# Delta rule of a hybrid encoder in fp32: where the projection's matmuls stand in levels 1 to 4 of the triangular inverse

## The reference

```python
proj = h @ w_in                                  # q, k, v, z of every head, and more
...
m = jnp.where(strict, jnp.einsum('bhncd,bhnsd->bhncs', k_beta, k) * decay, 0.0)
t_inv = lax.linalg.triangular_solve(eye + m, eye, lower=True, unit_diagonal=True, ...)
u = t_inv @ v_beta
w = t_inv @ (k_beta * jnp.exp(g)[..., None])
# then a scan over the chunks carries a 128 x 128 state through each head
```

## Time and profile before

| | us |
|---|---|
| median of 3 runs | 1468.76 (1468.46 to 1468.94) |
| the profiled execution | 1469.18 |
| its span, first to last instruction | 1467.4 |
| PE busy | 1424.6 (97% of the span) |
| DVE, ACT, POOL busy | 560.3, 579.1, 555.1 (38%, 39%, 38%) |

### The profile page before, as it was taken

One profiled execution on the slowest core, in us unless ns is written; L12 is line 12 of the kernel. 1 busy time (PEld: TensorE's weight loads), 2 busy tenths in 40 slices (PEclk: granted clock), 3 DMA queues, 4 the chain that ended last, 5 costly groups with the idle time before them and its releaser, 6 DMA issues.

```text
span 1467.4 us, 24342 instructions
## 1 busy us (share of the span) xinstructions
PE 1424.6 (97%) x9400; PEld 1146.5 (78%) x9400; DVE 560.3 (38%) x1054; ACT 579.1 (39%) x989; POOL 555.1 (38%) x270
## 2 busy tenths in 40 slices
PE   6989999999999999999999999999999999999998
PEld 6866777777776888888888887777788888888887
DVE  3555666666644322220122224774322221022210
ACT  5534554454435342322232335775333222222221
POOL 4533323223322443444344443222344434533432
PEclk9999999999999999999999999999999999999999
DMA  6322111111111332224323233111142323323232
GB/s 236 128 72 86 47 56 44 45 59 59 52 45 33 98 107 101 87 79 122 101 86 106 69 108 105 58 38 55 54 124 92 101 82 99 120 86 101 70 97 77
DMA packets 39230, 124.15 MB, mean 85 GB/s; under 512 B 4192, under 2 KB 5472, under 8 KB 39136
## 3 DMA queue, kind: packets, MB, share of 16 engines
q1 hardware_dynamic: 38976, 122.55, 26.2%
q10 hardware_dynamic: 160, 0.26, 0.1%
HBM read 120.44 MB, written 2.10 MB: 84 GB/s over the span
## 4 chain that ended last, share of the span: by engine, by line
PE 89%; DVE 6%; ACT 2%; issue 2%; DMA 0%; DVEq 0%; SPq 0%; ACTq 0%
PE bank L621 75%; DVE ws L1717 2%; DVE ws L1714 1%; ACT ws L1249 1%; PE bank L974 1%; PE bank L946 1%; PE bank L818 1%; DVE act_lo L1714 1%; PE bank L795 1%; PE bank L1181 1%; PE bank L633 1%; PE bank L1205 1%; PE bank L863 1%; PE bank L1192 1%; PE bank L837 0%
## 5 line engine op out<-in xcount | busy, mean ns | idle before, releaser
L563 POOL TENSOR_TENSOR w_lo<-w_raw,w_hi 128x1024 fp32r<-128x1024 f32 (+1 forms) x250 | 534.1, 2152 | 783.5 <-ACT w_hi L1249 783.5
L621 PE MATMUL bank<-act_hi,w_hi 128*128 128x512 f32 (+1 forms) x1776 | 709.8, 400 | 7.6 <-DVE act_lo L1714 2.6
L621 PE MATMUL bank<-act_hi,w_lo 128*128 128x512 f32 (+1 forms) x1776 | 680.7, 383 | 0.0
L621 PE MATMUL bank<-act_lo,w_hi 128*128 128x512 f32 (+1 forms) x1776 | 680.3, 383 | 0.0
L621 PEld LDWEIGHTS bank<-act_hi,w_hi 128*128 128x128 f32 x1776 | 335.6, 189 | 75.6 <-issue 7.3
L621 PEld LDWEIGHTS bank<-act_hi,w_lo 128*128 128x128 f32 x1776 | 335.4, 189 | 66.0
L621 PEld LDWEIGHTS bank<-act_lo,w_hi 128*128 128x128 f32 x1776 | 336.3, 189 | 58.7 <-issue 3.0
L1249 ACT ACTIVATE w_hi<-w_raw 128x1024 fp32r<-128x1024 f32 (+1 forms) x250 | 230.6, 953 | 92.7 <-PE bank L621 90.6
L1708 DVE TENSOR_TENSOR ws<-bank,ws 128x512 f32<-128x512 f32 x110 | 75.8, 690 | 335.1 <-PE bank L621 325.1
L1249 ACT ACTIVATE ws<-ws 128x512 f32<-128x512 f32 (+2 forms) x128 | 83.0, 650 | 156.7 <-DVE ws L1708 112.2
L2045 DVE TENSOR_TENSOR xT<-xT,bank 128x512 f32<-128x512 f32 (+1 forms) x48 | 33.0, 688 | 258.6 <-PE bank L621 258.6
(11 more groups left out here) (178 smaller groups left out, 969.6 us busy)
## 6 DMA issues: line engine op xcount, KB each, us to landing
w_raw<-w_stream SPq DMA_DIRECT2D x154, 512.0 KB, 3.3
w_raw<-w_out SPq DMA_DIRECT2D x32, 384.0 KB, 3.1
w_raw<-w_down SPq DMA_DIRECT2D x32, 384.0 KB, 3.1
w_raw<-w_down SPq DMA_DIRECT2D x32, 320.0 KB, 3.2
ws<-x_in SPq DMA_DIRECT2D x1, 2048.0 KB, 8.4
ws<-mem_in SPq DMA_DIRECT2D x2, 512.0 KB, 4.1
out<-ws SPq DMA_DIRECT2D x1, 1024.0 KB, 4.2
out<-ws SPq DMA_DIRECT2D x1, 768.0 KB, 3.6
```

Of the source, the lines that this page charges most:

```text
L563: nc.gpsimd.tensor_tensor(w_lo[:, s, 0:width * P], w_raw[:, s, 0:width * P], w_hi[:, s, 0:width * P].bitcast(F32), ALU.subtract).then_inc( ...
L621: mm = nc.tensor.matmul(acc, wt[:, c % RING, wsl], at[:, act0(k0 + k), off:off + n], start=(start and k == 0 and m == 0), stop=(stop and k ...
```

## The change

In levels 1 to 4 the dense portion between P and TZ is left out there, and both portions of the level are issued behind TZ. Levels 5 and 6 stay as they were. No instruction is added or removed, and no stream but TensorE's is touched.

```diff
                     mm.then_inc(S.p_mm, 1)
-                    fill(10 + 2 * k, 11 + 2 * k)
+                    if not quarters:
+                        fill(10 + 2 * k, 11 + 2 * k)
                     pe.wait_ge(S.p_done, P_PER_HEAD * h + (k if quarters else LEVELS - 1 if join else LEVELS))
...
                     mm.then_inc(S.tz_mm, 1)
-                    fill(11 + 2 * k, 12 + 2 * k)
+                    fill(10 + 2 * k if quarters else 11 + 2 * k, 12 + 2 * k)
```

## The result

The changed kernel takes 1476.71 us (median of 5 runs, 1474.94 to 1477.56) against 1468.76 us before (5 runs, 1468.46 to 1469.96). The ratio is 1.0051, with a 95% interval of 1.0038 to 1.0065: slower by 0.4 to 0.65%. The prediction was 1475.6 us.

What follows compares the result with a forecast made beforehand. TensorE, busy 1424.6 of 1467.4 us, was taken as the bound. Seven heads at 0.81 us and the last at 1.10 make 6.8 us; on the 1468.76 us median this gave 1475.6 us, range 1472.5 to 1479.5.

Steps and rivals of the forecast that it cites:

- P to TZ: Levels 1 to 4: TZ starts 0.53 + 0.29 + 0.05 = 0.87 us after P, where it came after 1.275.
- The level: Each of levels 1 to 4 becomes 0.275 us longer, 2.825 us instead of 2.55.
- the wait: Before TZ in levels 1 to 4, TensorE loses 0.49 us waiting for DVE's masking.
- the saved change of size: Levels 1 to 4: one change between small and large matmuls and back less, 0.21 us gained a level.
- The bound from below: Change of size may hide 0.11 us more; a level then costs 0.165 us, the whole 3.3 us.
- The tap: DVE's convolution tap no longer delays portion 16 in level 3 (0.21 us) or level 5's copies (0.08 us), in 7 heads.
- The changes of size: Rival at each TZ start: the wait is nothing and saved size changes make the kernel faster, 1460.1 us; 2%.
- given back later: Rival: TensorE's later idle times absorb the loss, no change, 1468.8 us or up to 2.9 above; 4%.
- The clock: Rival in the heads: new idle times drop TensorE's clock, 44 us beside the 6.8, about 1519 us; 3%.
- A longer way from DVE to TZ: Rival at TZ's start behind the masking: slower by a little more, 1478.8 us; part of the main case's spread.
- the bound from above: TZ may need up to 0.1 us more behind the masking, 3.2 us more, 10.0 us in all.
- level 1 to level 5: Expected sign in the profile: a head's span from level 1 to level 5 grows from 10.40 to about 11.1 us.

Runs made afterwards that it cites:

- e1: Changed kernel, but TZ in levels 1 to 4 reads the normalised keys and does not wait for the masking; 1462.18 us, 0.9950 of the kernel before.
- e6: Kernel before with the change made in level 2 alone; 1470.09 us, 1.0003 of the kernel before.
- e2: Kernel before, with both portions of levels 1 to 4 between P and TZ and none behind TZ; 1483.90 us, ratio 1.0096.
- e3: Kernel before, with one dense matmul between P and TZ in levels 1 to 4 and the other five behind TZ; 1469.29 us, ratio 1.0002.
- e11: e10 with POOL's third low part where it was in the kernel before; 1474.22 us, 1.0038 of the kernel before.
- e10: Kernel before, portions starting one earlier, a second one behind TZ of level 5, POOL's third low part after DVE's level 5 copies; 1461.10 us.
- e8: Kernel before, levels 3 and 4 without a portion between P and TZ, portions moved into levels 5 and 6; 1468.55 us, ratio 0.9996.
- e9: e8 with POOL's third low part of a head waiting for DVE's level 5 copies; 1465.42 us, 0.9975 of the kernel before.

## Why the prediction was right

**P to TZ.** 0.87 us predicted, 0.88 measured, 32 times, with the releaser named. It rested on rows of the same operations for the first two parts; the third, 0.05 us from DVE's end to TensorE's start, was borrowed from L803, another group of matmuls, and measured 0.06.

**The level.** 2.825 predicted, 2.85 measured. The step of dense matmuls behind TZ is 0.23 us and more, not 0.227, so that the second portion costs 0.70. Over four levels this makes 0.09 us a head and 0.7 us in all, by which the sum was low (7.5 us against 6.8).

**The split of the sum.** I had the wait at 0.49 us and the saved change of size at 0.21. By e1 they are 0.58 and 0.28. Their difference, which alone enters the sum, was right to 0.02 us (0.28 against 0.30). The bound from below was drawn for this case: it allowed the change of size 0.11 us more. But I had not seen that a larger value of the change makes the wait longer by as much, since TZ's start is set by DVE and not by what stood before it. The bound was therefore needlessly low.

**The tap.** 0.21 us in level 3 and 0.08 us at level 5, both as predicted (e6 shows the first alone, e2 what happens when the tap comes too late).

**The rivals.** The changes of size do not decide (e1, e3). Nothing is given back later: 7.40 us are still there at L1151. The clock did not fall in the heads of the changed kernel, in two profiles. That rival was nearer than I thought, though, because e1 and e11 with one idle time of 0.8 us instead of 0.4 have such stretches. A longer way from DVE to TZ was not seen: 0.06 us, with two waits or four. The 0.1 us that I had added for it in the bound from above came from no row.

**What I got wrong on the way.** I named 11.1 us for level 1 to level 5; my own terms give 4 x 2.825 = 11.3, and 11.38 was measured. And I took the profiled execution and the median for the same thing to 0.4 us; two executions of one kernel can differ by 1.7 us or more, most likely by a stretch of half clock that is there or not (no kernel has a profile of both kinds), and the change's own profile shows 5.8 us where the medians differ by 8.0 and 5.7. The changed kernel's two medians, 1476.71 and 1474.97, themselves lie 1.7 us apart, with 1475.6 between them. That the prediction came within 1.1 us of either is therefore partly luck. The better test is the heads' 7.5 us, the same in both profiles of the changed kernel, against 6.8.

## What to carry to other kernels

In a chain that goes back and forth between TensorE and DVE, dense work between two links is free only as cover: find for each gap how long the other engine needs from the start of one link (here 0.82 us), and put there enough to cover it. Such a gap cost 0.58 us of waiting when left open, and 0.28 us for the change of matmul size when covered; a single dense matmul in it covered the wait only in part and cost that change too (2.61 us a level in e3 against 2.55). Further dense work is worth more where the trace shows TensorE idle, and it is best taken from a run of dense work whose successor was ready long before, as in e10. When such a move fails, look at which long operation of another engine has come to lie over the critical one.

## What the runs showed of the hardware that I had not expected

- A POOL operation over 128x1024 elements (2.38 us) holds a 32x128 copy of DVE inside of SBUF until it ends: 0.85 us instead of 0.25 in e8, and six copies of 2.54 instead of 1.46 us in e11. DVE's two copies out of PSUM just ahead of them kept their 0.30 us under the same POOL operation in e8 (0.61 us for both, from 260.85). Only a part of this was tested: that moving POOL away restores the copy (e9, e10).
- A change between groups of 32x32 matmuls and 128x512 matmuls and back costs 0.28 us: a level with one such pair more takes 2.55 us against 2.27 in e1.
- TensorE's clock fell to 1.2 GHz for 3.4 us in 2 of the 6 heads of e1 and 3 of the 7 of e11 that have a wait of 0.8 us before L803, each time 2.1 to 2.6 us behind that wait and 0.2 to 0.7 us behind a second one of 0.3 us before the update of level 6, and in none of the changed kernel with its four waits of 0.42 us a head. What separates the two stays open. The stretch at about 903 us (902 to 918 in the longer kernels) is missing in 7 of the 14 profiles, though no edit touches what the kernel does there.
